# Token blocks 6 and 7 in row buffers of their own, blocks 2 to 5 made in one go, three low halves on VectorE

## The chip, the cores and the metric

The kernel runs on one core of a Trainium2 chip. The metric is the device time of one execution in microseconds (us). A token block is 128 tokens; a tile is one group of matrix products that fills one bank of PSUM.

## What is computed

One layer of a hybrid backbone: every token is normalised by its root mean square, modulated, and multiplied with one wide input matrix; what comes out feeds an mLSTM and a Hyena operator, and one output projection follows. The change touches the first lines of this alone:

```python
def rms_norm(x, g):
    xf = x.astype(jnp.float32)
    y = xf * lax.rsqrt(jnp.mean(xf * xf, axis=-1, keepdims=True) + RMS_EPS)
    return (y * g.astype(jnp.float32)).astype(x.dtype)
...
        hl = rms_norm(xl, pre_gain[l]) * (1.0 + scale_l[:, None]) + shift_l[:, None]
        hc = rms_norm(xc, pre_gain[l]) * (1.0 + scale_c) + shift_c
        qk_l, v_l, o_l, zm_l, g_l, hy_l, zh_l = split_proj(hl @ w_in[l])
        qk_c, v_c, o_c, zm_c, g_c, hy_c, zh_c = split_proj(hc @ w_in[l])
...
    uv = short_conv(u_hy, conv_w, conv_b, rows).astype(jnp.float32)
```

There are 256 context tokens (blocks 0 and 1) and 2048 latent tokens (blocks 2 to 17), each of 1024 channels.

## The kernel before

The input matrix is applied in three passes of TensorE, with tokens and weights split into a high and a low half (`h_hi`, `h_lo`, `w_hi`, `w_lo`; lines 511 to 513). The first tiles, `n` = 0 to 19, make the keys: tiles 0 to 3 are the four channel groups of the 256 context tokens, tiles 4 to 7 those of blocks 2 to 5, tiles 8 to 11 of blocks 6 to 9, tiles 12 to 15 of blocks 10 to 13, tiles 16 to 19 of blocks 14 to 17. So tile 4 needs the low halves of blocks up to 5, tile 8 up to 9, tile 12 up to 13 and tile 16 up to 17 (the wait on `lo_ready` in the tile loop of TensorE).

A block `j` is made while the tiles run, in these steps, each with its own semaphore:

- SyncE loads its rows (`load_x`, line 308) into a row buffer. From block 4 on there are two buffers (halves of `stage`), so block `j` is loaded when block `j - 2` has been turned.
- ScalarE squares and sums it (`square`, line 626), GpSimd takes the root in two small operations (`root`, lines 808 and 811), VectorE scales the rows (`normalise`, line 840).
- TensorE turns it into PSUM (`turn`, line 483), eight transposes; it also waits until block `j - 2` has been taken from the same bank.
- ScalarE and VectorE each take one half out of PSUM (`modulate`, lines 637 and 888). ScalarE rounds it to the high half (`high`, line 644), GpSimd subtracts for the low half (`low`, line 817); only block 1 has its low half from VectorE (line 895).

Every key tile goes out in further steps: ScalarE copies it from its bank (`conv_begin`, lines 669 and 671), VectorE adds the two outer taps of the short convolution (`taps`, lines 906 and 909), ScalarE applies the SiLU (`conv_end`, line 676), and SyncE stores it (`store`, line 348). Context tiles are 256 wide, the others 512.

Each engine works through its own list in the written order, and an instruction that waits holds up all behind it on that engine. In iteration `n` of ScalarE's loop stand `modulate(n + 3)`, `conv_end` of tile `n - 2`, `high(n + 3)`, `square(n + 5)`, `conv_begin` of tile `n`. SyncE's loop has in iteration `n` the load of block `n + 6`, which waits for the turn of block `n + 4`, and then the store of tile `n - 2`, which waits for that tile's `conv_end`. TensorE turns block `n + 3` behind tile `n`.

Of the kernel before, what the change touches and what calls it, by code (L numbers as in the profile page):

```python
# [24 lines left out]
F32 = mybir.dt.float32  # L25
# [97 lines left out]
def k_tile(n):  # L123

    return (n % 4,) + ([CTX_T] + LAT_T)[n // 4]
# [44 lines left out]
def project(nc, block, sem, d, s, svec, ident, hidden, opening, handed_banks):  # L170

    with ExitStack() as ctx:
# [7 lines left out]
        with nc.sbuf_tensor("mods", [P, N_MOD - 3, KD, SLOT], F32) as mods:  # L180
            pass
        h_hi = sb("h_hi", [P, KD, T_ALL], F32R)
        h_lo = sb("h_lo", [P, KD, T_ALL], F32R)
        work = sb("work", [P, 3 * D])
        cvec = sb("cvec", [P, KD, 2])
# [39 lines left out]

        def row_of(j):

            return j % 2 if j < 4 else 2 + j % 2

        rows = [work[:, 0:D], work[:, D:2 * D]] + \  # L230
            [stage[:, 2, :, :].rearrange("p k n -> p (k n)")[:, i * D:(i + 1) * D] for i in range(2)]

        bank = [ps(f"bank{i}", [P, TILE])[:, :] for i in range(4)] + handed_banks
        psM = bank[0][:, 0:4 * KD].rearrange("p (m s) -> p m s", s=2)
# [55 lines left out]

            return stage[:, c, :, :] if c < 3 else mods[:, c - 3, :, :]

        def rows_before(j):

            return sum(row_of(t) == row_of(j) for t in range(j + 1))

        def turned_behind(n):

            return (2, 3) if n == 0 else range(n + 3, min(n + 4, NT))

        def turned_bank(j, k):
            return bank[4 + 2 * (j % 2) + k // 4][:, k % 4 * P:(k % 4 + 1) * P]

        @block.sync
        def _(sp):
            def load_x(j):
                src = d["ctx"][j * P:(j + 1) * P, :] if j < NT_CTX else d["x"][(j - NT_CTX) * P:(j - NT_CTX + 1) * P, :]
                sp.dma_start(rows[row_of(j)], src).then_inc(x_loaded[row_of(j)], 16)

            sp.dma_start(cvec[:, :, :], d["cvec"]).then_inc(first_in, 16)  # L310
            sp.dma_start(ident[:, :], d["ident"]).then_inc(first_in, 16)
# [14 lines left out]
            sp.wait_ge(mod_used, 2)  # L326
            sp.dma_start(stage[:, 1, :, :], d["w_in"][1]).then_inc(w_loaded[1], 16)
            sp.wait_ge(mod_used, 3)
            load_x(4)
            load_x(5)  # L330

            def load_after(item, par):

# [75 lines left out]
                    sp.dma_start(s["cols"], cols).then_inc(cols_out, 16)  # L409

            for n in range(K_TILES + 2):
                if 6 <= n + 6 < NT:
                    sp.wait_ge(xt_ready, n + 5)
                    load_x(n + 6)
                if n >= 2:
                    m, t0, width = k_tile(n - 2)
                    store(silu_done, n - 1, by_chunk(s["k"], m, t0, width), (n - 2) % 4, width)
# [57 lines left out]
        def _(pe):  # L475

            def turn(j):
                pe.wait_ge(xhat_ready, j + 1)
                if j >= 2:
                    pe.wait_ge(ht_act, j - 1)  # L480
                    pe.wait_ge(ht_dve, j - 1)
                for k in range(KD):
                    mm = pe.transpose(turned_bank(j, k), rows[row_of(j)][:, k * P:(k + 1) * P], ident[:, :])
                mm.then_inc(xt_ready, 1)

            def turn_mod(row):
# [133 lines left out]
        def _(act):  # L620
# [1 line left out]
            act.activation(svec[:, :, :], cvec[:, :, :], ACT.Silu).then_inc(svec_ready, 1)  # L622

            def square(j):
                act.wait_ge(x_loaded[row_of(j)], 16 * rows_before(j))
                act.activation(h_lo[:, :, bass.ts(j, P)], rows[row_of(j)].rearrange("p (k t) -> p k t", k=KD),
                               ACT.Square, accum_out=sumsq[:, j:j + 1]).then_inc(ssq_ready, 1)

            def modulate(j):
                stream = int(j < NT_CTX)  # L630
                act.wait_ge(xt_ready, j + 1)
                if j == 0:
                    act.wait_ge(mod_step, 3)
                if j >= 2:
                    act.wait_ge(lo_ready, max(2, j - 1))
                for k in range(KD // 2):
                    ins = act.activation(ht[j % 2][:, k, :], turned_bank(j, k), ACT.Identity,
                                         bias=mod[:, k, stream:stream + 1], scale=gcol[:, k, stream:stream + 1])
                ins.then_inc(ht_act, 1)

            def high(j):
                act.wait_ge(ht_act, j + 1)
                act.wait_ge(ht_dve, j + 1)
                act.copy(h_hi[:, :, bass.ts(j, P)], ht[j % 2]).then_inc(hi_ready, 1)
# [53 lines left out]
            square(2)  # L698
            square(3)
            split(1, 1, 1, None)  # L700
            square(4)
            square(5)
            modulate(2)
            high(2)
            modulate(3)
            high(3)
            for n in range(K_TILES + 2):
                if 1 <= n and n + 3 < NT:
                    modulate(n + 3)
                if n >= 2:  # L710
                    conv_end((n - 2) % 4, n - 2, k_tile(n - 2)[2])
                if 1 <= n and n + 3 < NT:
                    high(n + 3)
                if 1 <= n and n + 5 < NT:
                    square(n + 5)
                if n < K_TILES:
                    if n == 0:
                        act.wait_ge(xt_ready, 4)
                    conv_begin(n, n % 4, n // 4, n, n % 2, k_tile(n)[2], k_tile(n)[0])
                if n == K_TILES - 2:  # L720
                    split(2, 0, 2, K_TILES - 2, P)
            split(3, 1, 2, K_TILES)
# [80 lines left out]
        @block.gpsimd  # L803
        def _(pool):

            def root(j):
                pool.wait_ge(ssq_ready, j + 1)
                pool.tensor_tensor(rstd[:, j:j + 1], sumsq[:, j:j + 1], power[:, 1:2], ALU.add)\
                    .then_inc(eps_added, 1)
                pool.wait_ge(eps_added, j + 1)  # L810
                pool.tensor_tensor(rstd[:, j:j + 1], rstd[:, j:j + 1], power[:, 0:1], ALU.pow)\
                    .then_inc(rstd_ready, 1)

            def low(j):
                tokens = bass.ts(j, P)
                pool.wait_ge(hi_ready, j + 1)
                pool.tensor_tensor(h_lo[:, :, tokens], ht[j % 2], h_hi[:, :, tokens].bitcast(F32), ALU.subtract)\
                    .then_inc(lo_ready, 1)

            pool.memset(power[:, 0:1], -0.5).then_inc(power_set, 1)  # L820
            pool.memset(power[:, 1:2], D * EPS).then_inc(power_set, 1)
            pool.wait_ge(power_set, 2)
            root(0)
            root(1)
            low(0)
            for j in range(2, 6):
                root(j)
            low(2)
            low(3)
            for j in range(4, NT):  # L830
                low(j)
                if j + 2 < NT:
                    root(j + 2)

        @block.vector
        def _(dve):
# [75 lines left out]
            modulate(0)  # L912
            modulate(1)
            split(0, 0, None)
            low(1)
            normalise(2)
            normalise(3)
# [2 lines left out]
            modulate(2)  # L920
            normalise(5)
            modulate(3)
            for n in range(K_TILES + 1):
                if 1 <= n and n + 3 < NT:
                    modulate(n + 3)
                if 2 <= n and n + 4 < NT:
                    normalise(n + 4)
                if n:
                    m, _, width = k_tile(n - 1)
                    taps(n - 1, (n - 1) % 4, n - 1, (n - 1) % 2, width, m, 1 if width == T_CTX else TILE // ROW)  # L930
                if n == K_TILES - 2:
                    split_gate()
            def accumulate_gate(c):
# [1830 lines left out]
```

## Time and profile before

| | us |
|---|---|
| median of 3 runs | 1582.09 (1578.92 to 1583.75) |
| profiled execution | 1580.21 |
| its span | 1578.4 |
| TensorE busy with products | 1529.7 (97% of the span) |
| VectorE, ScalarE, GpSimd busy | 712.1, 635.2, 309.5 |

The profiled execution lies 1.9 us below the median, and 1.8 us of it lie outside the span. TensorE is the engine to watch: where it waits, the kernel waits. All times below count from the start of the span. The profile gives for each instruction the start, the duration and, in brackets, how long its engine had been idle and who ended that.

### The profile page before, as it was taken

To read this page: it belongs to the slowest core of one execution; us is meant where nothing else is said; L and a number is where in the kernel's file an instruction comes from. 1 tells how busy PE (TensorE), PEld (TensorE's weight loads), DVE (VectorE), ACT (ScalarE), POOL (GpSimd) and SP (SyncE) were. 2 spreads that over 40 slices of the span, in tenths; PEclk is the share of its full clock that TensorE was granted. 3 is DMA by queue.
4 is the path that set the end of the run, shared out by engine and by line. 5 is a ranking of instruction groups with operands and counts; after the bars stand their busy time and mean duration, and the time that the engine had idled before them with its cause. 6 is when DMAs were issued, how large, how long until landed. Compare 5 with 4: busy or idle time off the path is not lost. (4 is left out here: it accounts for less than half of the span.)

```text
span 1578.4 us, 22997 instructions
## 1 busy us (share of the span) xinstructions
PE 1529.7 (97%) x8892; PEld 1340.5 (85%) x8892; DVE 712.1 (45%) x1127; ACT 635.2 (40%) x1360; POOL 309.5 (20%) x298
## 2 busy tenths in 40 slices
PE   5899999999999999999999999999999898999997
PEld 3788878888888888888888899999999887888886
DVE  1654430333333332201020287677775577676763
ACT  2785321433222222113121255555454386455551
POOL 0652000000000000000000021121313136756561
PEclk8899999999999999999999999999999999999999
DMA  8343621222212111212122365654535774656551
GB/s 349 101 114 87 204 101 49 85 74 74 80 73 73 73 56 70 100 48 106 47 77 74 122 219 141 187 137 108 149 89 165 252 251 146 214 184 216 183 184 54
DMA packets 128277, 201.92 MB, mean 128 GB/s; under 512 B 12572, under 2 KB 75794, under 8 KB 121271
## 3 DMA queue, kind: packets, MB, share of 16 engines
q1 hardware_dynamic: 128182, 200.64, 39.3%
q8 instruction: 62, 1.02, 0.3%
q14 instruction: 33, 0.26, 0.1%
HBM read 122.57 MB, written 52.86 MB: 111 GB/s over the span
## 5 line engine op out<-in xcount | busy, mean ns | idle before, releaser
L511 PE MATMUL bank<-h_hi,w_hi 128*128 128x512 f32 (+1 forms) x800 | 311.4, 389 | 11.1 <-DVE h_lo L895 9.2
L513 PE MATMUL bank<-h_hi,w_lo 128*128 128x512 f32 (+1 forms) x800 | 309.2, 386 | 0.0
L512 PE MATMUL bank<-h_lo,w_hi 128*128 128x512 f32 (+1 forms) x800 | 309.2, 386 | 0.0
L2151 POOL TENSOR_TENSOR prod<-prod,hidden 128x512 f32<-128x512 f32 x48 | 61.3, 1278 | 908.6 <-DVE hidden L2550 908.6
L511 PEld LDWEIGHTS bank<-h_hi,w_hi 128*128 128x128 f32 x800 | 151.5, 189 | 41.7 <-issue 10.0
L513 PEld LDWEIGHTS bank<-h_hi,w_lo 128*128 128x128 f32 x800 | 151.5, 189 | 30.3
L512 PEld LDWEIGHTS bank<-h_lo,w_hi 128*128 128x128 f32 x800 | 151.6, 190 | 29.7 <-issue 0.2
L906 DVE SCALAR_TENSOR_TENSOR work<-work,coef 128x504 f32<-128x504 f32 (+1 forms) x84 | 63.2, 752 | 237.2 <-ACT work L671 237.1
L511 PE MATMUL bank<-w_hi,h_hi 128*128 128x512 f32 (+1 forms) x448 | 164.5, 367 | 0.0
L512 PE MATMUL bank<-w_lo,h_hi 128*128 128x512 f32 (+1 forms) x448 | 164.1, 366 | 0.0
L513 PE MATMUL bank<-w_hi,h_lo 128*128 128x512 f32 (+1 forms) x448 | 164.1, 366 | 0.0
L661 ACT ACTIVATE work<-bank 128x512 f32<-128x512 f32 (+1 forms) x72 | 40.4, 562 | 296.8 <-PE bank L513 296.8
L669 ACT COPY work<-bank 128x512 f32<-128x512 f32 (+1 forms) x84 | 48.3, 575 | 231.2 <-PE bank L513 231.2
L847 DVE TENSOR_TENSOR w_lo<-stage,w_hi 128x2048 fp32r<-128x2048 f32 x18 | 41.2, 2291 | 216.9 <-ACT w_hi L651 214.3
L1504 PE MATMUL acc<-wo_hi,y_hi 128*128 128x512 f32 x256 | 103.0, 402 | 5.3 <-DVE late L1798 3.9
L1506 PE MATMUL acc<-wo_hi,y_lo 128*128 128x512 f32 x256 | 100.6, 393 | 0.0
L1505 PE MATMUL acc<-wo_lo,y_hi 128*128 128x512 f32 x256 | 100.4, 392 | 0.0
L511 PEld LDWEIGHTS bank<-w_hi,h_hi 128*128 128x128 f32 x448 | 84.5, 189 | 15.2 <-ACT work L661 0.9
L512 PEld LDWEIGHTS bank<-w_lo,h_hi 128*128 128x128 f32 x448 | 84.5, 189 | 13.8
L513 PEld LDWEIGHTS bank<-w_hi,h_lo 128*128 128x128 f32 x448 | 84.5, 189 | 13.8
L909 DVE SCALAR_TENSOR_TENSOR work<-work,coef 128x504 f32<-128x504 f32 (+1 forms) x84 | 63.6, 757 | 4.8 <-DVE work L906 2.4
L671 ACT ACTIVATE work<-bank,coef 128x512 f32<-128x512 f32 (+1 forms) x84 | 65.2, 777 | 0.0
(334 smaller groups left out, 2751.6 us busy)
## 6 DMA issues: line engine op xcount, KB each, us to landing
H<-spectrum SPq DMA_DIRECT2D x192, 128.0 KB, 2.3
stage<-in_w_in SPq DMA_DIRECT2D x18, 1024.0 KB, 5.5
s_hy<-work SPq DMA_DIRECT2D x48, 256.0 KB, 2.2
x<-s_hy SPq DMA_DIRECT2D x8, 1024.0 KB, 5.1
kq<-s_k SPq DMA_DIRECT2D x32, 256.0 KB, 4.7
v<-s_v SPq DMA_DIRECT2D x32, 256.0 KB, 5.5
mb<-s_rows SPq DMA_DIRECT2D x32, 256.0 KB, 4.9
late<-in_x SPq DMA_DIRECT2D x16, 512.0 KB, 7.1
```

The costliest lines, as they stand in the source:

```text
L511: pe.matmul(out, lhs[0], rhs[0], start=(k == 0), stop=False)
L512: pe.matmul(out, lhs[0], rhs[1], start=False, stop=False)
L513: return pe.matmul(out, lhs[1], rhs[0], start=False, stop=(k == KD - 1))
L669: act.copy(raw[r][:, 0:width], bank[slot][:, 0:width]).then_inc(raw_ready, 1)
L671: act.activation(res[slot][:, 0:width], bank[slot][:, 0:width], ACT.Identity, bias=bias, scale=w_mid).then_inc(bank_free, 1)
L847: dve.tensor_tensor(w_lo[:, par, :, 0:width], stage[:, par, :, 0:width], w_hi[:, par, :, 0:width].bitcast(F32), ALU.subtract).then_inc(w_l ...
L906: dve.scalar_tensor_tensor(y[:, :, 1:e], u[:, :, 0:e - 1], w_left, y[:, :, 1:e], ALU.mult, ALU.add).then_inc(tap_first, 1)
L909: dve.scalar_tensor_tensor(y[:, :, 0:e - 1], u[:, :, 1:e], w_right, y[:, :, 0:e - 1], ALU.mult, ALU.add).then_inc(tap_both, 1)
L1504: pe.matmul(o, y_hi[:, k, :], w_hi[:, k, cut], start=(k == HEADS), stop=False)
L1505: pe.matmul(o, y_hi[:, k, :], w_lo[:, k, cut], start=False, stop=False)
L1506: mm = pe.matmul(o, y_lo[:, k, :], w_hi[:, k, cut], start=False, stop=(k == HEADS - 1))
L2151: pool.tensor_tensor(cut, cut, crossed[:, t % 2], ALU.add).then_inc(added, 1)
```

## The change

Four things are changed, all in the opening:

- Blocks 6 and 7 get row buffers of their own (`ahead`, which lies where the low halves of blocks 16 and 17 will be written later) and are loaded right behind blocks 4 and 5. Blocks 8 and 9 follow into the two old buffers. Blocks that share a residue modulo 2 share one semaphore from block 4 on.
- TensorE turns blocks 4 and 5 behind tile 1, block 6 behind tile 2, and from there block `n + 4` behind tile `n`.
- ScalarE and VectorE make blocks 2 to 5 in one go before the outputs of tile 0. Then iteration `n` of ScalarE's loop is `conv_begin` of tile `n`, `square(n + 7)`, `modulate(n + 5)`, `conv_end` of tile `n - 1`, `high(n + 5)`; VectorE's is `taps` of tile `n`, `normalise(n + 7)`, `modulate(n + 5)`. Iterations 0 and 1 square blocks 8 and 9, and iteration 2 none.
- VectorE makes the low halves of blocks 0, 1 and 5, before only that of block 1. GpSimd makes the others.

SyncE's order of loads and stores is the same from block 10 on: the load of block `n + 6`, then the store of tile `n - 2`.

```diff
+        with nc.sbuf_tensor("ahead", [P, KD, T_ALL], F32) as ahead:
+            pass
...
-            return j % 2 if j < 4 else 2 + j % 2
+            return j % 2 if j < 4 else 4 + j % 2 if j in (6, 7) else 2 + j % 2
...
+            [ahead[:, :, bass.ts(NT - 2 + i, P)] for i in range(2)]
...
-            return (2, 3) if n == 0 else range(n + 3, min(n + 4, NT))
+            return {0: (2, 3), 1: (4, 5)}.get(n, range(n + 4, min(n + 5, NT)))
+        def squared_at(n):
+            return n + 8 if n < 2 else n + 7 if 3 <= n and n + 7 < NT else None
...
-            load_x(4)
-            load_x(5)
+            for j in range(4, 8):
+                load_x(j)
...
             for n in range(K_TILES + 2):
-                if 6 <= n + 6 < NT:
+                if n < 2:
+                    sp.wait_ge(xt_ready, n + 5)
+                    load_x(n + 8)
+                if 4 <= n and n + 6 < NT:
                     sp.wait_ge(xt_ready, n + 5)
                     load_x(n + 6)
...
-            square(4)
-            square(5)
-            modulate(2)
-            high(2)
-            modulate(3)
-            high(3)
-            for n in range(K_TILES + 2):
-                if 1 <= n and n + 3 < NT:
-                    modulate(n + 3)
-                if n >= 2:
-                    conv_end((n - 2) % 4, n - 2, k_tile(n - 2)[2])
-                if 1 <= n and n + 3 < NT:
-                    high(n + 3)
-                if 1 <= n and n + 5 < NT:
-                    square(n + 5)
+            for j in range(4, 8):
+                square(j)
+            for j in range(2, 6):
+                modulate(j)
+                high(j)
+            for n in range(K_TILES + 1):
                 if n < K_TILES:
...
                     conv_begin(n, n % 4, n // 4, n, n % 2, k_tile(n)[2], k_tile(n)[0])
+                if squared_at(n):
+                    square(squared_at(n))
+                if 1 <= n and n + 5 < NT:
+                    modulate(n + 5)
+                if n >= 1:
+                    conv_end((n - 1) % 4, n - 1, k_tile(n - 1)[2])
+                if 1 <= n and n + 5 < NT:
+                    high(n + 5)
...
-            low(0)
-            for j in range(2, 6):
+            for j in range(2, 8):
                 root(j)
             low(2)
             low(3)
-            for j in range(4, NT):
+            low(4)
+            root(8)
+            root(9)
+            for j in range(6, NT):
+                if 8 <= j < NT - 2:
+                    root(j + 2)
+                pool.wait_ge(lo_ready, j)
                 low(j)
...
             split(0, 0, None)
+            low(0)
             low(1)
...
-            for n in range(K_TILES + 1):
-                if 1 <= n and n + 3 < NT:
-                    modulate(n + 3)
-                if 2 <= n and n + 4 < NT:
-                    normalise(n + 4)
-                if n:
-                    m, _, width = k_tile(n - 1)
-                    taps(n - 1, (n - 1) % 4, n - 1, (n - 1) % 2, width, m, 1 if width == T_CTX else TILE // ROW)
+            normalise(6)
+            normalise(7)
+            modulate(4)
+            modulate(5)
+            dve.wait_ge(lo_ready, 5)
+            low(5)
+            for n in range(K_TILES):
+                m, _, width = k_tile(n)
+                taps(n, n % 4, n, n % 2, width, m, 1 if width == T_CTX else TILE // ROW)
+                if squared_at(n):
+                    normalise(squared_at(n))
+                if 1 <= n and n + 5 < NT:
+                    modulate(n + 5)
```

ScalarE, before: the row of block 8's `modulate` to the outputs of tile 5 (`keys`/`acc` is the PSUM bank of a turned block, `hidden`/`second` the buffer it is modulated into, `bank` that of a tile; the last operand is the shape).

```order
L637 ACTIVATE hidden<-keys,mod,gcol 128x128 x4
L676 ACTIVATE work<-work 128x256
L644 CAST h_hi<-hidden 128x8x128
L626 ACTIVATE h_lo,sumsq<-stage 128x8x128
L669 COPY work<-bank1 128x512
L671 ACTIVATE work<-bank1,coef 128x512
```

ScalarE, with the change: tile 3's outputs, the square of block 10, then block 8 and the outputs of tile 4.

```order
L682 COPY work<-bank3 128x256
L684 ACTIVATE work<-bank3,coef 128x256
L639 ACTIVATE h_lo,sumsq<-stage 128x8x128
L650 ACTIVATE hidden<-keys,mod,gcol 128x128 x4
L689 ACTIVATE work<-work 128x256
L657 CAST h_hi<-hidden 128x8x128
L682 COPY work<-bank0 128x512
L684 ACTIVATE work<-bank0,coef 128x512
```

The square of block 10 (`h_lo,sumsq<-stage`) stood behind `modulate(8)`, a SiLU and `high(8)`, and stands ahead of them now.

VectorE, before, from the low half of block 1 to the first taps of tile 0.

```order
L895 TENSOR_TENSOR h_lo<-second,h_hi 128x8x128
L840 TENSOR_SCALAR work<-work,rstd 128x1024 x2
L847 TENSOR_TENSOR w_lo<-stage,w_hi 128x2048
L840 TENSOR_SCALAR stage<-stage,rstd 128x1024
L888 TENSOR_SCALAR hidden<-keys,gcol,mod 128x128 x4
L840 TENSOR_SCALAR stage<-stage,rstd 128x1024
L888 TENSOR_SCALAR second<-acc,gcol,mod 128x128 x4
L888 TENSOR_SCALAR hidden<-keys,gcol,mod 128x128 x4
L906 SCALAR_TENSOR_TENSOR work<-work,coef 128x255
```

VectorE, with the change, from the low half of block 1 to the first taps of tile 0.

```order
L910 TENSOR_TENSOR h_lo<-second,h_hi 128x8x128
L855 TENSOR_SCALAR work<-work,rstd 128x1024 x2
L862 TENSOR_TENSOR w_lo<-stage,w_hi 128x2048
L855 TENSOR_SCALAR stage<-stage,rstd 128x1024
L903 TENSOR_SCALAR hidden<-keys,gcol,mod 128x128 x4
L855 TENSOR_SCALAR stage<-stage,rstd 128x1024
L903 TENSOR_SCALAR second<-acc,gcol,mod 128x128 x4
L855 TENSOR_SCALAR ahead<-ahead,rstd 128x8x128 x2
L903 TENSOR_SCALAR hidden<-keys,gcol,mod 128x128 x4
L903 TENSOR_SCALAR second<-acc,gcol,mod 128x128 x4
L910 TENSOR_TENSOR h_lo<-second,h_hi 128x8x128
L921 SCALAR_TENSOR_TENSOR work<-work,coef 128x255
```

Ahead of tile 0's taps VectorE now also normalises blocks 6 and 7, modulates block 5 and subtracts block 5's low half.

## Rows read from the trace of the kernel before

**Rows 1.** TensorE waits, 0 to 200 us: waiting line, releaser, us in total, times, longest.
```profile
PE bank L511 <- DVE h_lo L895: 9.2, 1, 9.2
...
PE bank L511 <- POOL h_lo L817: 2.0, 2, 1.8
PE keys L483 <- DVE stage L840: 1.2, 1, 1.2
```

**Rows 2.** TensorE timeline: start, duration (us), engine, line, operation, count, idle before.
```profile
43.84 0.55 PE L511 MATMUL bank<-h_hi,w_hi 128*128 128x256 f32 x1 [9.17 <-DVE h_lo L895]
...
48.45 1.03 PE L483 MATMUL keys<-ident,work 128*128 128x128 f32 x8
...
61.91 1.09 PE L483 MATMUL keys<-ident,stage 128*128 128x128 f32 x8 [1.20 <-DVE stage L840]
64.80 0.76 PE L511 MATMUL bank<-h_hi,w_hi 128*128 128x512 f32 x1 [1.79 <-POOL h_lo L817]
...
71.89 1.04 PE L483 MATMUL acc<-ident,stage 128*128 128x128 f32 x8
...
91.72 0.48 PE L511 MATMUL bank<-h_hi,w_hi 128*128 128x512 f32 x1
...
117.12 0.48 PE L511 MATMUL bank<-h_hi,w_hi 128*128 128x512 f32 x1
...
142.04 0.47 PE L511 MATMUL bank<-h_hi,w_hi 128*128 128x512 f32 x1 [0.16 <-POOL h_lo L817]
```

**Rows 3.** Stretches: busy time and instructions of each engine, PEclk the granted clock.
```profile
43.84:47.60 3.76, 3.76 (x17) 3.76 (x18) 2.75 (x3) 2.52 (x5) 3.60 (x6) 0.50 0.01 4
60.43:64.80 4.37, 1.38 (x12) 0.97 (x10) 3.66 (x3) 4.37 (x11) 3.06 (x4) 0.99 0.22 38
64.80:68.00 3.20, 3.20 (x8) 2.52 (x9) 2.95 (x8) 2.60 (x5) 1.32 (x3) 0.50 0.48 173
72.00:142.00 70.00, 69.88 (x353) 58.42 (x351) 37.82 (x77) 55.23 (x108) 34.89 (x29) 1.00 0.39 107
```

**Rows 4.** VectorE timeline, 40 to 82 us (columns as in rows 2).
```profile
40.44 3.25 DVE L895 TENSOR_TENSOR h_lo<-second,h_hi 128x1024 fp32r<-128x1024 f32 x1
...
45.61 0.75 DVE L840 TENSOR_SCALAR work<-work,rstd 128x1024 f32<-128x1024 f32 x1 [0.45 <-POOL rstd L811]
...
49.52 1.36 DVE L888 TENSOR_SCALAR hidden<-keys,gcol,mod 128x128 f32<-128x128 f32 x4 [0.30 <-PE keys L483]
...
55.96 1.39 DVE L906 SCALAR_TENSOR_TENSOR work<-work,coef 128x255 f32<-128x255 f32 x1
...
61.77 0.48 DVE L906 SCALAR_TENSOR_TENSOR work<-work,coef 128x255 f32<-128x255 f32 x1
...
81.24 0.74 DVE L906 SCALAR_TENSOR_TENSOR work<-work,coef 128x504 f32<-128x504 f32 x1
```

**Rows 5.** GpSimd timeline, 39 to 142 us.
```profile
39.54 3.07 POOL L817 TENSOR_TENSOR h_lo<-hidden,h_hi 128x1024 fp32r<-128x1024 f32 x1 [28.03 <-ACT h_hi L644]
...
45.81 0.96 POOL L811 TENSOR_TENSOR rstd<-rstd,power 128x1 f32<-128x1 f32 x1
...
52.18 2.39 POOL L817 TENSOR_TENSOR h_lo<-hidden,h_hi 128x1024 fp32r<-128x1024 f32 x1 [2.55 <-ACT h_hi L644]
54.67 2.40 POOL L817 TENSOR_TENSOR h_lo<-second,h_hi 128x1024 fp32r<-128x1024 f32 x1
...
60.52 0.55 POOL L811 TENSOR_TENSOR rstd<-rstd,power 128x1 f32<-128x1 f32 x1
...
139.48 2.42 POOL L817 TENSOR_TENSOR h_lo<-second,h_hi 128x1024 fp32r<-128x1024 f32 x1 [3.67 <-ACT h_hi L644]
```

**Rows 6.** ScalarE timeline around blocks 10 and 9.
```profile
83.29 1.06 ACT L626 ACTIVATE h_lo<-stage 128x1024 fp32r<-128x1024 f32 x1 [1.24 <-DMA stage<-in_x]
...
85.64 1.51 ACT L637 ACTIVATE second<-acc,mod,gcol 128x128 f32<-128x128 f32 x4
87.02 0.65 ACT L676 ACTIVATE work<-work 128x512 f32<-128x512 f32 x1
87.54 1.06 ACT L644 CAST h_hi<-second 128x1024 fp32r<-128x1024 f32 x1
```

**Rows 7.** SyncE timeline: the load of block 10, then a store.
```profile
79.29 0.33 SPq L308 DMA_DIRECT2D stage<-in_x  x1
79.66 0.43 SPq L348 DMA_DIRECT2D s_k<-work  x1
```

**Rows 8.** Line 308 (loads of token blocks), 50 to 130 us: issue to landing.
```profile
DMA to landing us min/median/max: 3.5/4.1/4.4
```

More of the change, by code:

```diff
@@ L226, in row_of @@
         def row_of(j):
-            return j % 2 if j < 4 else 2 + j % 2
+            return j % 2 if j < 4 else 4 + j % 2 if j in (6, 7) else 2 + j % 2
         rows = [work[:, 0:D], work[:, D:2 * D]] + \
             [stage[:, 2, :, :].rearrange("p k n -> p (k n)")[:, i * D:(i + 1) * D] for i in range(2)]
+        rows = [row.rearrange("p (k t) -> p k t", k=KD) for row in rows] + \
+            [ahead[:, :, bass.ts(NT - 2 + i, P)] for i in range(2)]
         bank = [ps(f"bank{i}", [P, TILE])[:, :] for i in range(4)] + handed_banks
@@ L291, in mod_weights, with load_of @@
             return stage[:, c, :, :] if c < 3 else mods[:, c - 3, :, :]
-        def rows_before(j):
-            return sum(row_of(t) == row_of(j) for t in range(j + 1))
+        def load_of(j):
+            return (j % 2, j // 2 + 1) if j < 4 else (2 + j % 2, max(2, j // 2 - 1))
         def turned_behind(n):
-            return (2, 3) if n == 0 else range(n + 3, min(n + 4, NT))
+            return {0: (2, 3), 1: (4, 5)}.get(n, range(n + 4, min(n + 5, NT)))
+        def squared_at(n):
+            return n + 8 if n < 2 else n + 7 if 3 <= n and n + 7 < NT else None
         def turned_bank(j, k):
@@ L307, in load_x @@
                 src = d["ctx"][j * P:(j + 1) * P, :] if j < NT_CTX else d["x"][(j - NT_CTX) * P:(j - NT_CTX + 1) * P, :]
-                sp.dma_start(rows[row_of(j)], src).then_inc(x_loaded[row_of(j)], 16)
+                sp.dma_start(rows[row_of(j)], src.rearrange("p (k t) -> p k t", k=KD)).then_inc(x_loaded[load_of(j)[0]], 16)
             sp.dma_start(cvec[:, :, :], d["cvec"]).then_inc(first_in, 16)
@@ L482, in turn @@
                 for k in range(KD):
-                    mm = pe.transpose(turned_bank(j, k), rows[row_of(j)][:, k * P:(k + 1) * P], ident[:, :])
+                    mm = pe.transpose(turned_bank(j, k), rows[row_of(j)][:, k, :], ident[:, :])
                 mm.then_inc(xt_ready, 1)
@@ L624, in square @@
             def square(j):
-                act.wait_ge(x_loaded[row_of(j)], 16 * rows_before(j))
-                act.activation(h_lo[:, :, bass.ts(j, P)], rows[row_of(j)].rearrange("p (k t) -> p k t", k=KD),
+                loads, count = load_of(j)
+                act.wait_ge(x_loaded[loads], 16 * count)
+                act.activation(h_lo[:, :, bass.ts(j, P)], rows[row_of(j)],
                                ACT.Square, accum_out=sumsq[:, j:j + 1]).then_inc(ssq_ready, 1)
@@ L829, in _ @@
             low(3)
-            for j in range(4, NT):
+            low(4)
[5 more added lines that the diff above has]
+                pool.wait_ge(lo_ready, j)
                 low(j)
-                if j + 2 < NT:
-                    root(j + 2)
         @block.vector
```

## The prediction

> **What bounds the kernel now.** I read four views in this order. The waits of TensorE come first, since it is busy 97% of the span and any wait of it is paid in full. Behind the loading of the weights they show 9.2 us before the first product with `h_lo`, 2.0 us for a low half of GpSimd, and 1.2 us for a `normalise` of VectorE [rows 1]. The timeline places them: tile 0 starts at 43.84, the turn of block 6 waits 1.20 us (61.91), tile 4 waits 1.79 us (64.80) [rows 2]. The granted clock adds to both. It stays at 0.50 (1.2 of 2.4 GHz) until 47.6, and again from 64.80 to 68.0, behind a stretch of 4.37 us in which TensorE had 1.38 us of work [rows 3]. From 72 to 142 us TensorE is busy 69.88 of 70.00 us at clock 1.00 [rows 3]: there is nothing to win there, only to lose. Four tiles and four turns take 117.12 - 91.72 = 25.4 us, so one pair takes 6.35 us [rows 2].
>
> The edit can win at most this: tile 3 ended at 61.91 - 1.20 = 60.7; a turn (0.8) and a wide tile (5.55) without wait would end at 67.0, where tile 4 now ends at 71.89 [rows 2]. That is 4.9 us, and about 0.6 from an earlier tile 0.
>
> **Tile 0.** GpSimd's low half of block 0 runs from 39.54 for 3.07 us, to 42.61 [rows 5]; VectorE's of block 1 is issued at 40.44, takes 3.25 us and ends 1.1 us after GpSimd's [rows 4]. So alone it would take some 1.15 us, and the rest was waiting for the other engine's. Two in a row on VectorE, with GpSimd idle, end at 40.4 + 2.3 = 42.7, and tile 0 starts at 42.8 instead of 43.84. Half of this is lost, for these products run at the half clock until 47.6 anyway [rows 3]: tile 0 ends at about 48.0 instead of 48.45.
>
> **Blocks 2 to 7.** From 48.45 to 60.7 TensorE makes three narrow tiles and four turns, so a narrow tile is 3.0 us [rows 2]. With both turns behind tile 1, tile 2 ends at 56.9 and the turn of block 6 could follow. It needs block 4 out of the bank. ScalarE takes a block in 2.5 us, `modulate` 1.5 and `high` 1.06 [rows 6]; with block 2 turned at 48.9, `high(2)` ends at 51.6 and `high(3)` at 54.1. GpSimd's `low(2)`, 2.4 us [rows 5], runs from 51.7 to 54.1. VectorE has meanwhile ended `modulate(3)` at 52.4 and comes to `normalise(6)`. Whether that can run beside `low(2)` no row shows. What the rows show is the reverse: GpSimd's root, 0.55 us when alone, took 0.96 us while VectorE normalised (0.75 us from 45.61) [rows 4, 5]; and VectorE's taps, 0.48 us alone, took 1.39 us behind a GpSimd low half, and ended just behind it [rows 4, 5]. The bounds are no wait and a full one. I take the full one, as nearest to these rows. Then `normalise(6)` ends at 54.7, `low(3)` is held until 54.5 and ends at 56.9, `normalise(7)` waits for it, and `modulate(4)` (1.36 us [rows 4]) ends at 58.8. The turn of block 6 waits 2 us and tile 3 ends at 62.5, the turn of block 7 at 63.3. `high(4)` ends at 59.9, GpSimd's `low(4)` at 62.3, VectorE's `low(5)` at 63.6, so tile 4 starts at 63.7, at the full clock, and ends at 69.2 against 71.89, with one more turn done. If `normalise` runs beside `low`, all of this and what follows lies 3.2 us earlier.
>
> The Trainium skill, page "SBUF — State Buffer", section "Who interferes with whom", says that VectorE and GpSimd share a pair of ports as an exclusive lock, that `tensor_scalar` in its two-port mode and any operation with two SBUF inputs take it, and that the later one blocks until the other ends. By that rule the full wait holds; the taps row agrees.
>
> **The loop that the new order closes.** This is the largest term. In the new iteration of ScalarE `square(n + 7)` stands ahead of `conv_end(n - 1)`. SyncE issues the store of tile `n - 1` only after that `conv_end`, and the load of block `n + 8` only after that store. So each load waits for the square of the block loaded before it: load, square, `modulate`, SiLU, store, next load. Before, `conv_end` of the tile to be stored stood ahead of the waiting square, and a load waited for nothing but its turn. One lap, for wide tiles: from issue of the load to the square 4.0 us (79.29 to 83.29 [rows 6, 7]; landings 3.5 to 4.4, median 4.1 [rows 8], which I take), square 1.06, `modulate` 1.4, SiLU 0.65 [rows 6], store's issue 0.43 [rows 7], semaphores 0.1: **7.7 us, where TensorE needs 6.35**. In the laps with a narrow tile it is 0.2 less.
>
> The lap starts at the load of block 10. ScalarE ends `high(5)` at 62.4, the outputs of tiles 0 and 1 and two squares at 66.0, waits for VectorE's `modulate(6)` (69.3, behind `low(5)`, two taps pairs, two `normalise`) and ends `high(6)` at 70.4, then the outputs of tile 2, `modulate(7)` and the SiLU of tile 1 at 72.9; the store goes at 72.9, the load at 73.4. Block 8 has been turned at 70, so it isn't TensorE that holds this load. It is still 5.9 us ahead of today's 79.29 [rows 7]. From here I add laps: load 11 at 81.0, load 15 at 112.0, load 17 at 127.5.
>
> **What tile 8, 12 and 16 wait for.** `modulate(9)` of VectorE stands behind `normalise(11)`, and so behind load 11. From load 11: square after 4.2, its root and the wake-up of VectorE 2.3 (with a wait for the taps), `normalise` 0.7, `modulate` 1.4, `high` 1.06, `low` 2.4 [rows 4 to 6], together 12.1 us: `low(9)` ends at 93.1. Tile 8 started at 91.72 [rows 2]: **1.4 us late**. Block 13 hangs in the same way on load 15: 112.0 + 12.1 = 124.1, where tile 12 started at 117.12 [rows 2]: **7.0 late**. Blocks 16 and 17 have no load behind them. `high(15)` ends at 137.0, 9.5 us behind load 17; two rounds follow in which the taps, issued 1.2 us behind the `high`, wait for the `low` (2.4), then taps 1.5 (two of 0.74 [rows 4]), `modulate` 1.4, `high` 1.06, 6.3 each; `low(17)` ends at 149.6 + 2.5 = 152.1. Today it ends at 139.48 + 2.42 = 141.9 and tile 16 starts at 142.04 [rows 2, 5]: **10.1 late**. TensorE has by then waited some 3 us in one piece three times; behind such a wait today the clock was 0.50 for 3.20 us, half of which is lost [rows 3]. The lateness of tile 16 holds earlier waits and their clock, so only the last one adds: 1.6 us. Tiles 16 to 19 are as before, and what follows is bound by TensorE.
>
> Sum: 10.1 + 1.6 = 11.7 us later. Against the profiled execution 1580.2 + 11.7 = 1591.9 us; the median of the runs lies 1.9 higher, so 1593.8, rounded **1594 us**.
>
> The other edits cost nothing: the extra loads of blocks 6 and 7 go behind all that is needed first, and their squares, behind those of blocks 4 and 5, come at 45 to 47.5, before block 2 is turned; if they landed up to 1.5 us later than that, nobody would wait.
>
> **Bounds.** The landing enters eight times (seven laps and the last). At the shortest, 3.5 us, the sum falls by 0.6 x 8 = 4.8 to 6.9. In the new order the store is ahead of the load, which no row shows; a store's packets could add up to some 0.8 us, which makes 11.7 + 6.4 = 18. Without the wait of `normalise` the sum is 8.5. A measurement of this kernel can tell about 0.3%, 4.7 us, from no change.
>
> **Rivals.**
> - *The same loop, cheaper*: `normalise` runs beside `low`, or the laps are somewhat shorter: 1582.1 + 8.5 = 1590.6. For it: GpSimd's low half is not seen to hold a `normalise`. Against: the taps row. Chance 0.18.
> - *The same loop, dearer*: the loads land behind the stores, 1582.1 + 17 = 1599. Chance 0.12.
> - *Faster*: the lap is shorter than TensorE's 6.35 us and the loop never binds. Then the opening keeps 4.9 + 0.6 = 5.5: 1576.6. The point from which it decides is a landing of 4.1 - 1.35 = 2.75 us. The shortest of all is 3.5 [rows 8]. Chance 0.06.
> - *No difference*: gain and loss cancel. With landings of about 3.4 and no wait of `normalise`, 11.7 - 3.2 - 5.6 = 2.9: 1585. Chance 0.07.
>
> **Chances.** The forecast has 0.57. Faster by over 0.3%: 0.06, within 0.3%: 0.07, slower: 0.87. The range, 1586 to 1600, takes in both bounds of the landing but for their last us, and leaves out the faster and most of the equal case.
>
> **What would show it.** In the profile after: tile 0 starting near 42.8; TensorE waiting about 2 us for the turn of block 6; loads of blocks 11 to 17 spaced 7.5 to 7.8 us, each right behind a store, where now they are 6.35 apart and ahead of it; tiles 8, 12 and 16 each waiting for GpSimd's `h_lo`, with clock 0.50 for some us behind it; tile 16 near 152. If the loads are 6.35 us apart, the loop isn't there and I am wrong in sign. If they are 7.7 apart and the time is unchanged, then blocks reach TensorE by less slack than I think, and the 12.1 us from a load to the low half two blocks back is the step that failed.

## The result

The changed kernel takes 1589.62 us (median, 1587.21 to 1591.35) where the kernel before, run beside it, takes 1581.71 (1578.92 to 1583.75). The ratio is 1.0049, with a 95% interval from 1.0037 to 1.0061: **7.9 us slower**, where 1594 (11.9 slower) was forecast. The profiled execution of the changed kernel is its fastest, 1587.21 us with a span of 1585.4: 7.0 more than before in both.

The page of the kernel after: the span, the busy time of TensorE and VectorE, and two groups of instructions (busy, mean ns of one, idle time before them with what ended most of it). Lines have moved: 511 to 523 (products), 483 to 495 (turns), 817 to 829 (GpSimd's low half), 840 to 855 (`normalise`), 888 to 903 (VectorE's `modulate`), 895 to 910 (its low half), 906 to 921 (the first of a pair of taps).

```profile
span 1585.4 us, 23010 instructions
PE 1529.8 (96%) x8892; PEld 1340.8 (85%) x8892; DVE 726.2 (46%) x1129; ACT 635.0 (40%) x1360; POOL 309.0 (19%) x296
L523 PE MATMUL bank<-h_hi,w_hi 128*128 128x512 f32 (+1 forms) x800 | 312.6, 391 | 15.9 <-DVE h_lo L910 8.1
L921 DVE SCALAR_TENSOR_TENSOR work<-work,coef 128x504 f32<-128x504 f32 (+1 forms) x84 | 75.0, 892 | 268.5 <-ACT work L684 268.5
```

TensorE's work is the same, 1529.8 us against 1529.7, and the span is longer: it waits more. VectorE's busy time is 14 us longer, mostly without more work: the 84 taps of line 921 take 892 ns on average where the page of the kernel before has 752 (84 x 0.14 = 11.8 us), and two `normalise` take 5.1 us. "Busy" counts time in which an instruction is held, and these are held.

TensorE waits of the kernel after, 0 to 200 us (line, releaser, us in total, times, longest), which answer to [rows 1]:

```profile
PE bank L523 <- DVE h_lo L910: 8.1, 1, 8.1
PE bank L523 <- POOL h_lo L829: 7.6, 3, 3.6
PE keys L495 <- DVE hidden L903: 1.5, 1, 1.5
...
PE acc L495 <- DVE second L903: 0.7, 1, 0.7
```

TensorE timeline of the kernel after, the instructions behind which these waits stand, and the first product of the stage that follows (line 565); it answers to [rows 2]:

```profile
39.67 0.55 PE L523 MATMUL bank<-h_hi,w_hi 128*128 128x256 f32 x1 [8.15 <-DVE h_lo L910]
...
55.53 1.06 PE L495 MATMUL keys<-ident,ahead 128*128 128x128 f32 x8 [1.52 <-DVE hidden L903]
...
85.92 0.84 PE L495 MATMUL acc<-ident,stage 128*128 128x128 f32 x6 [0.69 <-DVE second L903]
...
89.54 0.77 PE L523 MATMUL bank<-h_hi,w_hi 128*128 128x512 f32 x1 [2.56 <-POOL h_lo L829]
...
119.39 0.47 PE L523 MATMUL bank<-h_hi,w_hi 128*128 128x512 f32 x1 [1.47 <-POOL h_lo L829]
...
146.82 0.77 PE L523 MATMUL bank<-h_hi,w_hi 128*128 128x512 f32 x1 [3.60 <-POOL h_lo L829]
...
170.18 0.28 PE L565 MATMUL bank<-h_hi,w_lo 128*128 128x256 f32 x1
```

The wait of tile 4 is gone, and that of the turn of block 6 is 1.52 us instead of 1.20. New are the waits of tiles 8, 12 and 16 for a low half of GpSimd, 2.56, 1.47 and 3.60 us, and 0.69 at the turn of block 11. Stretches of the kernel after (busy time of PE, PEld, DVE, ACT and POOL, granted clock, share of the DMA engines, GB/s), which answer to [rows 3]:

```profile
39.67:44.20 4.53, 4.53 (x21) 4.53 (x22) 3.52 (x3) 4.53 (x8) 3.57 (x4) 0.50 0.39 118
72.00:142.00 70.00, 65.29 (x311) 53.92 (x310) 43.15 (x65) 48.55 (x96) 36.50 (x26) 0.95 0.29 87
89.54:95.40 5.86, 5.86 (x14) 4.60 (x15) 3.17 (x7) 3.61 (x8) 2.44 (x3) 0.50 0.43 134
146.82:150.00 3.18, 3.18 (x8) 2.53 (x9) 2.62 (x5) 2.19 (x5) 0.00 (x0) 0.50 0.41 123
```

From 72 to 142 us, where nothing was to be won, TensorE is now busy 65.29 us and not 69.88, and behind the waits of tiles 8 and 16 it works at clock 0.50 (1.2 GHz) for 5.86 and 3.18 us. From these rows and those of before, the way to the first product of line 565 adds up as follows (half of a stretch at clock 0.50 is lost):

| us, profiled executions | before | after |
|---|---|---|
| tile 0 starts | 43.84 | 39.67 |
| half clock behind it | 3.76 / 2 = 1.9 | 4.53 / 2 = 2.3 |
| waits behind tile 0's start | 1.20 + 1.79 + 0.16 = 3.2 | 1.52 + 0.69 + 2.56 + 1.47 + 3.60 = 9.8 |
| half clock behind a wait | 3.20 / 2 = 1.6 | (5.86 + 3.18) / 2 = 4.5 |
| what is left: products and turns | 113.4 | 113.9 |
| first product of line 565 | 163.93 | 170.18 |

So 9.6 us of new waits and of clock lost behind them, and 0.8 in the two other rows, stand against a start 4.2 us earlier, of which 1.0 is the change's doing (last section). Of the 7.0 us of the span, 6.25 have arisen at this point.

### The profile page after: what moved, and what is told of

The parts are those of the page before. It is cut to its first block and busy times, and to the rows that moved or that the text cites. A ratio compares the mean times of both kernels' runs of the same rounds, so it can differ in the third digit from the quotient of the medians.

```text
span 1585.4 us, 23010 instructions
## 1 busy us (share of the span) xinstructions
PE 1529.8 (96%) x8892; PEld 1340.8 (85%) x8892; DVE 726.2 (46%) x1129; ACT 635.0 (40%) x1360; POOL 309.0 (19%) x296
## 5 line engine op out<-in xcount | busy, mean ns | idle before, releaser
L921 DVE SCALAR_TENSOR_TENSOR work<-work,coef 128x504 f32<-128x504 f32 (+1 forms) x84 | 75.0, 892 | 268.5 <-ACT work L684 268.5
L682 ACT COPY work<-bank 128x512 f32<-128x512 f32 (+1 forms) x84 | 48.3, 575 | 230.3 <-PE bank L525 230.2
L924 DVE SCALAR_TENSOR_TENSOR work<-work,coef 128x504 f32<-128x504 f32 (+1 forms) x84 | 61.5, 732 | 4.8 <-DVE work L921 2.4
```

Of the source, the lines that this page charges most:

```text
L682: act.copy(raw[r][:, 0:width], bank[slot][:, 0:width]).then_inc(raw_ready, 1)
L921: dve.scalar_tensor_tensor(y[:, :, 1:e], u[:, :, 0:e - 1], w_left, y[:, :, 1:e], ALU.mult, ALU.add).then_inc(tap_first, 1)
L924: dve.scalar_tensor_tensor(y[:, :, 0:e - 1], u[:, :, 1:e], w_right, y[:, :, 0:e - 1], ALU.mult, ALU.add).then_inc(tap_both, 1)
```

## Why the blocks come late: two loops

SyncE timeline of the kernel after, three rounds; it answers to [rows 7]:

```profile
76.39 0.36 SPq L357 DMA_DIRECT2D s_k<-work  x1
76.79 0.47 SPq L317 DMA_DIRECT2D stage<-in_x  x1
83.70 0.36 SPq L357 DMA_DIRECT2D s_k<-work  x1
84.11 0.47 SPq L317 DMA_DIRECT2D stage<-in_x  x1
91.05 0.36 SPq L357 DMA_DIRECT2D s_k<-work  x1
91.45 0.50 SPq L317 DMA_DIRECT2D stage<-in_x  x1
```

The loads stand right behind stores, as predicted. From block 10 (69.60) to block 17 (121.28) there are seven laps of 51.68 / 7 = 7.38 us, where TensorE takes a block every 6.35.

The other engines show a second loop. Timelines of the kernel after: ScalarE, GpSimd, VectorE, from one `high` (line 657) to the next. Line 639 is the square, 820 and 823 are the root, 921 and 924 a pair of taps.

```profile
85.87 1.05 ACT L657 CAST h_hi<-second 128x1024 fp32r<-128x1024 f32 x1 [2.19 <-DVE second L903]
86.82 0.58 ACT L682 COPY work<-bank 128x512 f32<-128x512 f32 x1
87.29 0.78 ACT L684 ACTIVATE work<-bank,coef 128x512 f32<-128x512 f32 x1
87.97 1.05 ACT L639 ACTIVATE h_lo<-stage 128x1024 fp32r<-128x1024 f32 x1
...
93.28 1.04 ACT L657 CAST h_hi<-hidden 128x1024 fp32r<-128x1024 f32 x1 [2.25 <-DVE hidden L903]
```

```profile
87.05 2.34 POOL L829 TENSOR_TENSOR h_lo<-second,h_hi 128x1024 fp32r<-128x1024 f32 x1 [3.34 <-ACT h_hi L657]
89.35 0.63 POOL L820 TENSOR_TENSOR rstd<-sumsq,power 128x1 f32<-128x1 f32 x1
90.07 1.06 POOL L823 TENSOR_TENSOR rstd<-rstd,power 128x1 f32<-128x1 f32 x1
```

```profile
88.18 1.76 DVE L921 SCALAR_TENSOR_TENSOR work<-work,coef 128x504 f32<-128x504 f32 x1 [2.40 <-ACT work L684]
89.97 0.74 DVE L924 SCALAR_TENSOR_TENSOR work<-work,coef 128x504 f32<-128x504 f32 x1
91.16 0.76 DVE L855 TENSOR_SCALAR stage<-stage,rstd 128x1024 f32<-128x1024 f32 x1 [0.44 <-POOL rstd L823]
91.83 1.36 DVE L903 TENSOR_SCALAR hidden<-keys,gcol,mod 128x128 f32<-128x128 f32 x4
```

The square at 87.97 has no bracket: it waits for no load. Yet the lap is 93.28 - 85.87 = 7.41 us. One step follows the other: `high` ends at 86.9, GpSimd's low half at 89.4; the first taps, ready at 88.2, end only at 89.9 and the second at 90.7; the root, queued behind the low half, takes 1.06 us beside these taps where it takes 0.55 alone, and ends at 91.1; then `normalise`, then `modulate`, and only then the next `high`. This **ring through the compute engines** holds no DMA, and is as long as the loop through SyncE. The trace alone can't say which of the two sets the pace.

## The experiments

Seven kernels ran, the first four and the last three each as one group with the kernel before beside them (medians 1581.12 and 1582.06 us). Each ratio is to that kernel before, and kernels are compared by these ratios. "After" in an edit is the changed kernel.

The profiles give a second measure: the time from the start of tile 0 to the first product of the stage behind the key tiles (line 553 or 565). It leaves out the differences ahead of tile 0. The clock of 0.50 behind tile 0 lasts 3.1 to 5.8 us in these profiles, so the last column is without the half of it that is lost. Each row is one profile.

| kernel | ratio to the kernel before | tile 0 to the next stage, us | half clock behind tile 0, us | without its loss, us |
|---|---|---|---|---|
| before | 1 | 120.1 | 3.8 | 118.2 |
| after | 1.0049 | 130.5 | 4.5 | 128.2 |
| one store later | 1.006 | 131.4 | 3.1 | 129.9 |
| modulate first | 1.0018 | 122.2 | 3.2 | 120.6 |
| both | 0.9971 | 117.6 | 5.7 | 114.7 |
| both, two low halves on VectorE | 0.9952 | 115.0 | 4.3 | 112.8 |
| low half of block 0 alone | 0.9985 | 120.3 | 4.0 | 118.3 |
| two low halves, loops kept | 1.0042 | 127.5 | 5.8 | 124.6 |
| normalise last | 0.9974 | 118.9 | 3.8 | 117.1 |

### One store later on SyncE

After, with the store of tile `n - 3` in place of that of tile `n - 2`: no load waits for the square of the block before it.

```diff
-            for n in range(K_TILES + 2):
+            for n in range(K_TILES + 3):
...
-                if n >= 2:
-                    m, t0, width = k_tile(n - 2)
-                    store(silu_done, n - 1, by_chunk(s["k"], m, t0, width), (n - 2) % 4, width)
+                if n >= 3:
+                    m, t0, width = k_tile(n - 3)
+                    store(silu_done, n - 2, by_chunk(s["k"], m, t0, width), (n - 3) % 4, width)
```

> The changed kernel, with each store of a key tile issued one iteration later by SyncE, so that a load no longer stands behind the store whose SiLU waits for the square of the block before. Theory A (the loop over SyncE alone sets the lap of 7.4 us): laps fall to TensorE's 6.35 us, tiles 8, 12 and 16 hardly wait, 1576 to 1580 us. Theory B (a second ring of equal length through ScalarE, VectorE and GpSimd: high, low, taps, root, normalise, modulate, high, 7.41 us in the trace after): laps stay at 7.4 us, the time stays within 1.5 us of the changed kernel, near 1589.

Measured: 1589.62 us (1588.02 to 1595.66), ratio 1.006 [1.0042, 1.0078]. Nothing was won. SyncE timeline of this kernel, then what waited for the loads (line 317, 50 to 135 us; no engine is named) and their landing:

```profile
75.31 0.33 SPq L317 DMA_DIRECT2D stage<-in_x  x1
77.88 0.38 SPq L357 DMA_DIRECT2D s_k<-work  x1
81.67 0.33 SPq L317 DMA_DIRECT2D stage<-in_x  x1
...
who waited for it (us, times):
busy tenths in 40 slices 0000000000000000000000000000000000000000
DMA to landing us min/median/max: 3.5/3.7/4.5
```

The loop is cut, the loads come ahead of the stores, and no engine waits for one. Yet TensorE waits where it did; its waits for GpSimd in this kernel:

```profile
PE bank L523 <- POOL h_lo L829: 8.7, 3, 3.6
```

One `high` follows the other as before, at 87.75 and 95.17, 7.42 us apart. The loop that the prediction put all on can be removed without any effect.

### The modulate first on VectorE

After, with another order in VectorE's iteration: the ring is shortened, the loop through SyncE stays.

```diff
                 m, _, width = k_tile(n)
+                if 1 <= n and n + 5 < NT:
+                    modulate(n + 5)
                 taps(n, n % 4, n, n % 2, width, m, 1 if width == T_CTX else TILE // ROW)
                 if squared_at(n):
                     normalise(squared_at(n))
-                if 1 <= n and n + 5 < NT:
-                    modulate(n + 5)
```

> The changed kernel, with VectorE's iteration in the order modulate, taps, normalise instead of taps, normalise, modulate, so that the high half no longer waits for the root and the normalise of the block two later, nor for taps that wait for GpSimd. The loop over SyncE is left. Theory A: laps stay at 7.2 to 7.4 us; some us are won all the same, because the low half of a block comes earlier against its load: near 1585 us (1583 to 1587). Theory B alone: laps fall to 6.35 us and the time to 1576 to 1580.

Measured: 1584.5 us (1581.13 to 1586.04), ratio 1.0018 [1.0008, 1.0028]. Tiles 8 and 16 wait no more, tile 12 waits 2.64 us. ScalarE timeline of this kernel:

```profile
89.40 1.06 ACT L639 ACTIVATE h_lo<-stage 128x1024 fp32r<-128x1024 f32 x1 [2.15 <-DMA stage<-in_x]
```

Now the square waits 2.15 us for a load, and ScalarE waits for loads eight times, 19.9 us in all. The loads are 7.1 to 7.6 us apart (78.45, 85.58, 92.89, 100.32): without the ring the loop through SyncE sets the pace. Shortening the ring won about 5 us, and left a kernel that is still slower than before.

### Both

After with both edits.

> Both edits of the two runs above. If the two loops together are the cause of the loss, laps are 6.35 us, tiles 8, 12 and 16 wait for nothing or under 1 us, and the kernel is faster than the one before: 3 to 5 us below it, 1577 to 1579. If something else holds the laps, it stays near 1589.

Measured: 1576.72 us (1574.39 to 1581.94), ratio 0.9971 [0.9959, 0.9984]: 4.6 us faster than the kernel before. A stretch of this kernel and its only wait of TensorE behind tile 0 until the end of these tiles:

```profile
72.00:142.00 70.00, 70.00 (x346) 58.65 (x345) 49.10 (x76) 54.58 (x106) 33.41 (x27) 1.00 0.36 104
```

```profile
PE keys L495 <- DVE hidden L903: 1.5, 1, 1.5
```

The loads are 6.35 us apart (77.57, 83.93, 90.27), TensorE's own step; ScalarE still waits 10.5 us for loads in all, and TensorE for none of it. One edit alone won nothing, the other about 5 us (1.0049 to 1.0018); both win 12.3 (1.0049 to 0.9971). Two loops of nearly one length lay side by side, and each was enough to hold TensorE up. Against this kernel, which has neither, the loop through SyncE alone costs 7.4 us (0.9971 to 1.0018), the ring alone 14 (to 1.006), both 12.3; the last two are one within their intervals.

### Both, and two low halves on VectorE

The kernel of the last experiment, with the low halves of blocks 2 and 3 taken from GpSimd to VectorE, so that no `normalise` meets a low half of GpSimd.

```diff
+            low(2)
             normalise(6)
             normalise(7)
             modulate(4)
+            low(3)
             modulate(5)
...
-            low(2)
-            low(3)
+            pool.wait_ge(lo_ready, 4)
             low(4)
```

> As the run above, and the low halves of blocks 2 and 3 made by VectorE instead of GpSimd, so that the normalise of blocks 6 and 7 finds no low half of GpSimd running. If that collision (5.13 us for two normalise that take 1.4 alone) is what TensorE waits for ahead of the turn of block 6, that wait (1.5 us) goes and the time is 2 to 3 us below the run above; if VectorE becomes late instead, it is the same or worse.

Measured: **1573.82 us** (1572.48 to 1574.59), ratio 0.9952 [0.9935, 0.9968], the fastest of all, 7.6 us below the kernel before by the ratio. VectorE timeline of the kernel after, then of this kernel, the two `normalise` of blocks 6 and 7:

```profile
48.98 5.13 DVE L855 TENSOR_SCALAR ahead<-ahead,rstd 128x1024 f32<-128x1024 f32 x2
```

```profile
50.68 1.21 DVE L909 TENSOR_TENSOR h_lo<-hidden,h_hi 128x1024 fp32r<-128x1024 f32 x1
51.81 1.40 DVE L854 TENSOR_SCALAR ahead<-ahead,rstd 128x1024 f32<-128x1024 f32 x2
```

Beside GpSimd's low halves (48.35 to 50.75 and 50.83 to 53.56 in the kernel after) the pair takes 5.13 us, without them 1.40. The turn of block 6 waits no more, and TensorE has no wait behind tile 0 until the stage of line 565. Against the last experiment the step is 2.9 us by the medians; with five runs of this kernel the intervals just overlap. The last column of the table gives 1.9.

### The low half of block 0 alone

The kernel before with `low(0)` on VectorE ahead of `low(1)`, and nothing else changed.

```diff
-            low(0)
...
             split(0, 0, None)
+            low(0)
             low(1)
```

> The kernel before with one edit: the low half of block 0 by VectorE instead of GpSimd. From the low halves alone tile 0 starts 1.0 us earlier; since its products run at the half clock until the clock rises, 0.5 us should reach the end, 1580.6 against about 1581.1. If the change had another gain hidden in this edit (the 1.7 us by which the changed kernel lost less than the reckoning with its measured laps), it would show as 2 us here.

Measured: 1580.37 us (1577.73 to 1585.66), ratio 0.9985 [0.9973, 0.9997]: 0.5 to 4.3 us faster (the medians are 1.7 apart). VectorE timeline of this kernel, the two low halves:

```profile
40.06 1.23 DVE L894 TENSOR_TENSOR h_lo<-hidden,h_hi 128x1024 fp32r<-128x1024 f32 x1
41.19 1.23 DVE L894 TENSOR_TENSOR h_lo<-second,h_hi 128x1024 fp32r<-128x1024 f32 x1
```

They take 2.36 us together, where the one of before took 3.25 behind GpSimd's [rows 4]. By the runs the sign is sure, and the size isn't: it could be the 0.5 of the prediction or the 2.4 in the middle. The profiles are finer. TensorE's wait ahead of tile 0 is 9.17 us in the kernel before and 8.14 to 8.15 in all eight kernels with this edit, so tile 0 comes 1.0 us earlier. The half clock behind it ended at 46.54 here and not at 47.60, so the profile doesn't show the loss of half of that gain which was expected: from tile 0 on, this kernel is only 0.2 us longer than the one before (120.3 against 120.1).

### Two low halves on VectorE, the loops kept

After, with the low halves of blocks 2 and 3 on VectorE, as in the experiment before the last, and nothing else: both loops stay.

> The changed kernel with the low halves of blocks 2 and 3 on VectorE and both loops left in place. The collision of normalise and low half was worth 2.9 us where nothing waited behind it. If the gain simply adds, 1586.7; if the loops swallow most of it, because a lap of 7.4 us starts from wherever it is released, 1587 to 1589.

Measured: 1588.56 us (1585.53 to 1592.76), ratio 1.0042 [1.0029, 1.0055]. TensorE waits of this kernel:

```profile
PE bank L523 <- POOL h_lo L829: 5.8, 3, 2.6
PE acc L495 <- DVE second L902: 1.6, 2, 0.9
PE keys L495 <- DVE hidden L902: 0.4, 1, 0.4
```

The turn of block 6 has no wait; tiles 8, 12 and 16 and three turns still have theirs. By the ratios this kernel is 1.1 us faster than the changed one, within intervals that hold no gain as well as one of 2.9 us, so the runs don't decide whether the loops swallow the gain. The profiles speak against it: tiles 8, 12 and 16 start 48.3, 78.2 and 105.6 us behind tile 0, where the changed kernel has 49.9, 79.7 and 107.2. Each is 1.5 us earlier, as much as the wait at the turn of block 6 was. The loops start earlier too: the load of block 10 goes 28.4 us behind tile 0 instead of 29.9. At the next stage it is 3.0 us (127.5 against 130.5): the wait of tile 16, 0.71 us instead of 3.60, has no half clock behind it here.

### The normalise last, the taps first

After with the later store, and in VectorE's iteration taps, `modulate`, `normalise`: of the ring only the link through root and `normalise` is taken out.

```diff
-                if squared_at(n):
-                    normalise(squared_at(n))
                 if 1 <= n and n + 5 < NT:
                     modulate(n + 5)
+                if squared_at(n):
+                    normalise(squared_at(n))
```

> The changed kernel with stores one iteration later and VectorE in the order taps, modulate, normalise: the modulate, and with it the high half, is free of the root and the normalise, but still stands behind taps that wait for GpSimd's low half. It cuts one link of the engines' ring and leaves the other. If the link through root and normalise makes the lap long, it lies near the run with both cut (1576.7), about 2 us above: 1578 to 1579.5. If the collision of taps and low half alone holds the lap, it stays at 1589.

Measured: 1579.64 us (1574.82 to 1583.02), ratio 0.9974 [0.9962, 0.9985]. By the ratio it is 4.1 us faster than before (the medians are 2.4 apart) and not to be told from the kernel with both edits (0.9971). Its waits for GpSimd, where the one with the later store alone has 8.7 us:

```profile
PE bank L523 <- POOL h_lo L829: 1.4, 2, 1.0
```

Its `high`s are 6.28 us apart (98.82, 105.10), where the changed kernel has 7.41. So it is the `normalise` ahead of the `modulate`, with the root behind a low half and beside the taps, that makes the ring longer than TensorE's step of 6.35. What is left of the ring, through the taps, is just shorter than that step, and 1.4 us of waits remain. By the last column of the table this kernel lies 2.4 us behind the one with both edits (117.1 against 114.7); the runs can't tell them apart.

## The prediction, point by point

- **What bounds, and what could be won: right.** From 72 to 142 us there was nothing to win for TensorE [rows 3]. The opening has its gain once the loops are gone: without them the change is 4.6 us faster (2.5 to 6.5 by its interval), where the rival *faster* had 5.5, and 7.6 with two more low halves moved.
- **Tile 0: right, its effect less sure.** Two low halves in 2.35 us (37.18 to 39.53), 2.3 said. Tile 0 waits 1.0 us less, as said. Alone the edit wins 0.5 to 4.3 us by the runs, so the 0.5 to 0.6 is at the lower edge; that the products of tile 0 run at the half clock until 47.6 anyway didn't hold in the profile of that kernel (46.54).
- **`normalise` against GpSimd's low half: right.** The full wait was taken, from the row of the taps. The pair took 5.13 us, and the turn of block 6 waited 1.52 us with 2 said. A slip explains the rest: from tile 0's end at 48.0, four turns of 0.8 and two tiles of 3.0 end at 57.2 and not at 56.9, and the wait would be 1.6. Priced at 3.2 us; the kernels with and without it are 2.9 apart by the medians. The rule that the prediction cites from the Trainium skill, page "SBUF — State Buffer", section "Who interferes with whom", agrees with these rows.
- **Tile 4: right.** It waits no more and starts at 60.48, 20.8 us behind tile 0; 20.9 was said (63.7 - 42.8).
- **The lap: the step that was mis-sized.** 7.7 us were said, 7.38 measured: from the load of block 10 to that of block 17 it is 51.68 us where the prediction has 127.5 - 73.4 = 54.1. These 2.4 us are over half of the 4.2 by which the forecast (1593.8 before rounding) is too high. In the lap from 84.11 to 91.45 the square starts 3.86 us behind the load's issue (4.1 said) and the next load goes 0.40 behind the store (0.53 said); the rest is as said. The landing was 3.9 us in the median (3.6 to 4.5 seen), and the square waited for it only 0.3 and 0.2 us in the first two laps: after them the load was no longer what was late.
- **The cause: half missed.** The prediction gave the lateness to SyncE's loop alone. It even priced a lap of the ring, 6.3 us, for the two rounds behind load 17 (6.27 measured, from the `low` at 131.79 to that at 138.06). It never asked how long this lap is in the rounds before, where root and `normalise` stand in it as well: 7.41. The experiments show that the loop through SyncE is real and enough for a slower kernel (2.8 us with the `modulate` first), but that the ring alone brings the whole loss (the later store), and both together no more than the ring. The number came out nearly right by luck: both laps are nearly 7.4 us long.
- **From a load to the low half of two blocks back: nearly right.** Load 11 goes at 76.79 and `low(9)` ends at 89.39: 12.6 us, 12.1 said. Most of the difference lies between the start of the square (80.83) and the `normalise` (83.75): 2.9 us, where 2.3 were put for root and wake-up, and the square itself (1.06) has no term of its own. Beside the taps the root's two operations take 0.52 and 1.06 us here. From load 17 (121.28) to the start of tile 16 it is 25.5, where the prediction had 24.6.
- **Where TensorE waits: right.** Tiles 8, 12 and 16, with 2.56, 1.47 and 3.60 us instead of three times 3. The clock of 0.50 came behind the first and the last; behind the last it cost 1.6 us, as said.
- **The store ahead of the load: the upper bound did not come.** It had up to 0.8 us a lap, for which no row was given; landings were 3.6/3.9/4.5 us where [rows 8] have 3.5/4.1/4.4.
- **The sum.** From the start of tile 0 to that of tile 16: 98.20 us before, 109.3 forecast, 107.15 measured. In the profiled execution tile 16 is at 146.82 and not 152.1: 2.15 us by that, and 3.1 since tile 0 began at 39.67 and not at 42.8. The latter is an accident of this execution: with the same instructions ahead of it tile 0 began as late as 43.30 in another.
- **Open.** Of the 4.2 us between forecast and median, 2.15 lie between tile 0 and tile 16; the other 2 have no shown cause. They are no more than the measurement leaves open: without the 2.15 the forecast is 9.6 us above the kernel before, and the interval of the ratio ends at 9.6.

## To carry to other kernels

When an edit changes the order on in-order engines, follow every closed ring of "this waits for that, and stands in the queue behind it", sum each lap, and compare each with the bottleneck's period. There may be several, and one through a DMA is the easiest to see and not always the one that binds: here the removal of one of two nearly equal loops changed nothing (1589.62 us with it and without it), that of the other won 5 us and left a kernel slower than before, and only both gave 1576.72. So an edit that wins nothing doesn't acquit the loop that it removes. Price the lap of every round, not of the last ones alone: a step that stands in the ring in some rounds only, here root and `normalise`, made the difference between 6.3 and 7.4 us.

## What was not expected

**The start of tile 0 differs by 3.6 us between executions of the same instructions, with TensorE's clock.** While the weights are loaded, TensorE works in small pieces. Stretches of the kernel before, then of the kernel after, from the fall of the granted clock to tile 0 (columns as above):

```profile
23.70:43.84 20.14, 8.94 (x64) 5.16 (x57) 8.77 (x15) 11.18 (x18) 4.22 (x3) 0.50 0.75 302
```

```profile
20.00:30.60 10.60, 6.86 (x89) 4.13 (x85) 0.00 (x0) 1.75 (x3) 0.00 (x0) 1.00 1.01 421
30.60:39.67 9.07, 0.93 (x5) 0.86 (x5) 7.78 (x16) 8.96 (x16) 1.18 (x2) 0.50 1.05 395
```

The clock fell at 23.7 us in one and at 30.6 in the other, and tile 0 began at 43.84 and 39.67. Of these 4.2 us, 1.0 is the shorter wait for the low halves; the rest came before it. Sixteen of the small products take 1.07 us at clock 1.00 and 1.93 at 0.50, and the last of them can't start until those ahead of it are done. The other profiles:

| kernel | clock fell, us | tile 0, us |
|---|---|---|
| one store later | 27.6 | 41.59 |
| modulate first | 25.7 | 42.96 |
| both | 25.1 | 43.30 |
| both, two low halves on VectorE | 21.8, back at 28.6 | 41.37 |
| low half of block 0 alone | 22.7 | 42.56 |
| two low halves, loops kept | 25.0 | 43.07 |
| normalise last | 26.4 | 43.18 |

The two kernels in which it fell last start tile 0 first and third. The time of the fall alone doesn't order the others: in one it fell first of all and tile 0 was second, since the clock came back in between. The work ahead of tile 0 is the same in all but the kernel before and the one with `low(0)` alone. A single pair of profiles therefore can't be compared by the clock time of an event at this scale; the distance from tile 0 can, within the half clock behind it. Why the clock falls at different times for the same instructions wasn't tried.

**GpSimd's small operations are held by VectorE too.** The root's second operation, 128 x 1 elements, takes 0.55 us alone and 1.06 beside the taps, seven times in a row in the kernel after (from 82.65 to 127.38; 0.80 in the round before). Such small work would be thought free, and here it stood in the ring.
